# Two FFNs on inputs scaled by the norm's weight alone, the norm's factor applied per token to the gate and up tiles

## The reference, cut to what matters

```python
def rms_norm(x, g):
    xf = x.astype(jnp.float32)
    y = xf * lax.rsqrt(jnp.mean(xf * xf, axis=-1, keepdims=True) + RMS_EPS)
    return (y * g.astype(jnp.float32)).astype(x.dtype)

def swiglu(h, w1, w3, w2):                       # 1024 -> 2816 (gate w1, up w3) -> 1024
    return (jax.nn.silu(h @ w1) * (h @ w3)) @ w2

x = x + 0.5 * swiglu(rms_norm(x, ffn1_norm), ffn1_w1, ffn1_w3, ffn1_w2)      # FFN 1
... # the mixer: projections, RWKV recurrence, attention, gates
x = x + (gate_a * y_a + gate_b * y_b) @ w_out
x = rms_norm(x + 0.5 * swiglu(rms_norm(x, ffn2_norm), ffn2_w1, ffn2_w3, ffn2_w2), final_norm)   # FFN 2
... # the second block, with FFN 3 and FFN 4
```

## Time and profile before

| | |
|---|---|
| runs | 1651.48, 1647.41, 1649.91 us; median 1649.91 |
| the profiled execution | 1648.0 us, span 1646.2 us, mean granted clock 0.997 |
| PE busy | 1627.7 us, 99% of the span |
| DVE busy | 1115.4 us, 68% |
| ACT busy | 698.3 us, 42% |
| POOL busy | 23.9 us, 1% |
| HBM read | 265.38 MB, 162 GB/s over the span |
| chain that ended last | PE 73%, issue 23%, DVE 3%, ACT 1% |
| FFN 1 | about 12 to 204 us |
| output projection | about 452 to 477 us |
| FFN 2 | about 481 to 668 us |

### The profile page before, as it was taken

How to read it: one execution, slowest core, us unless ns; L and a number is a source line. 1 busy time by engine, 2 the same in 40 slices (tenths; PEclk the granted TensorE clock), 3 DMA queues, 4 the chain that set the end, 5 groups by cost and what they waited for, 6 DMA issues and landing times.

```text
span 1646.2 us, 30278 instructions
## 1 busy us (share of the span) xinstructions
PE 1627.7 (99%) x12552; PEld 1477.9 (90%) x12552; DVE 1115.4 (68%) x1617; ACT 698.3 (42%) x918; POOL 23.9 (1%) x41
## 2 busy tenths in 40 slices
PE   9999999999999999999999999999999999999998
PEld 7999888899999999988888887988999999999997
DVE  7666657564887766668887874967457676676665
ACT  6444456434455444421222122516354445454443
POOL 1000000000000000000000000000000000000000
PEclk9999999999999999999999999999999999999998
DMA  7555477322265545243456542233323355545551
GB/s 292 178 188 194 154 283 265 120 79 105 104 237 180 203 178 195 98 158 140 164 193 253 193 166 77 103 128 104 108 77 112 146 183 187 194 154 189 192 180 52
DMA packets 37837, 267.80 MB, mean 163 GB/s; under 512 B 4268, under 2 KB 4524, under 8 KB 5744
## 3 DMA queue, kind: packets, MB, share of 16 engines
q1 hardware_dynamic: 33552, 238.25, 40.5%
q0 software_dynamic: 4192, 28.19, 4.5%
HBM read 265.38 MB, written 1.05 MB: 162 GB/s over the span
## 4 chain that ended last, share of the span: by engine, by line
PE 73%; issue 23%; DVE 3%; ACT 1%; DMA 0%; POOL 0%; POOLq 0%; SPq 0%; DVEq 0%; ACTq 0%
PE PS L436 15%; PE PS L437 15%; PE PS L442 11%; PE PS L655 9%; PE PS L828 6%; PE PS L659 5%; PE PS L684 2%; PE PS L892 1%; DVE W_LO L430 1%; PE PS L540 1%; PE PS L872 1%; PE PS L874 1%; PE PS L873 1%; PE PS L1178 0%; PE PS L1353 0%
## 5 line engine op out<-in xcount | busy, mean ns | idle before, releaser
L430 DVE TENSOR_TENSOR W_LO<-RAW,W_HI 128x2048 fp32r<-128x2048 f32 x210 | 476.2, 2269 | 181.8 <-ACT W_HI L418 180.9
L418 ACT ACTIVATE W_HI<-RAW 128x2048 fp32r<-128x2048 f32 x208 | 397.6, 1913 | 362.1 <-PE PS L442 239.9
L436 PE MATMUL PS<-HS,W_HI 128*128 128x256 f32 (+1 forms) x792 | 265.3, 339 | 1.5 <-ACT G L1732 0.8
L437 PE MATMUL PS<-HS,W_LO 128*128 128x256 f32 (+1 forms) x792 | 261.5, 334 | 0.0
L655 PE MATMUL PS<-HS,W_HI 128*128 128x512 f32 x984 | 246.5, 392 | 0.7 <-DVE W_LO L430 0.7
L442 PE MATMUL PS<-HS,W_HI 128*128 128x512 f32 (+1 forms) x712 | 242.1, 340 | 0.0
L436 PE MATMUL PS<-HID_HI,W_HI 128*128 128x256 f32 (+1 forms) x720 | 220.6, 307 | 0.3 <-DVE XC L2598 0.3
L437 PE MATMUL PS<-HID_HI,W_LO 128*128 128x256 f32 (+1 forms) x720 | 220.2, 307 | 0.0
L655 PEld LDWEIGHTS PS<-HS,W_HI 128*128 128x128 f32 x984 | 177.0, 189 | 32.6 <-DVE W_LO L430 0.9
L436 PEld LDWEIGHTS PS<-HS,W_HI 128*128 128x128 f32 x792 | 150.1, 189 | 19.7 <-issue 3.3
L437 PEld LDWEIGHTS PS<-HS,W_LO 128*128 128x128 f32 x792 | 150.2, 190 | 14.9
(11 more groups left out here) (442 smaller groups left out, 2425.6 us busy)
## 6 DMA issues: line engine op xcount, KB each, us to landing
RAW<-stream SPq DMA_DIRECT2D x225, 1024.0 KB, 4.8
LATE<-stream POOLq DMA_DIRECT2D x24, 1024.0 KB, 5.1
XC<-xin SPq DMA_DIRECT2D x2, 512.0 KB, 4.6
XC<-xin POOLq DMA_DIRECT2D x1, 1024.0 KB, 5.1
out<-NT SPq DMA_DIRECT2D x4, 256.0 KB, 2.6
CON<-consts POOLq DMA_DIRECT2D x1, 616.0 KB, 6.5
LW<-lora POOLq DMA_DIRECT2D x1, 512.0 KB, 6.7
DFT<-dft POOLq DMA_DIRECT2D x1, 266.0 KB, 2.9
```

Of the source, the lines that this page charges most:

```text
L418: nc.scalar.activation(W_HI[s % RING][:], RAW[PLACE[u]][:], ACT.Copy).then_inc(hi_done, 1)
L430: last = nc.vector.tensor_tensor(W_LO[s % RING][:, o], RAW[PLACE[u]][:, o], W_HI[s % RING][:, o].bitcast(F32), ALU.subtract)
L436: nc.tensor.matmul(acc, w_hi, x_hi, start=first, stop=False)
L437: return nc.tensor.matmul(acc, w_lo, x_hi, start=False, stop=last)
```

## The change

In FFN 1 and FFN 2 the matmuls take `x * g`, split into high and low part straight from `XC`; the factor per token is copied once from its PSUM spread to SBUF (`RSF`, `RSC`) and multiplied on DVE onto every gate sum and every up sum (`by_rms`). On the last tile the silu is multiplied once more by the factor in place of the up half. For FFN 1 the rows are made by DVE, eight scalings and eight remainders; the square adds go to POOL, and unit 0's low part goes from POOL to DVE, in halves. For FFN 2 ACT makes the high row `k` behind add `k` and before square `k`, and DVE the low row `m - 1` before add `m`. On PE, the norm sums and the spread move into the first up tile, whose passes are reordered; the sums, scalings, roundings and `keep_clock` matmuls ahead of FFN 2 go, and the wait for `mod_out` moves from before up 2 to before FFN 2. The third and fourth FFN stay as they are.

```diff
@@ gpsimd
-            pool.wait_ge(landed[0], 16)
-            for h in range(2):
-                pool.wait_ge((S("hi_half"), hi_done)[h], 1)
-                ...
-            last.then_inc(lo_done, 1)
+            for k in range(1, NORM_ADDS["na"] + 1):
+                pool.wait_ge(S("norm_sq"), k + 1)
+                if k > 1:
+                    pool.wait_ge(S("norm_acc"), k - 1)
+                nc.gpsimd.tensor_tensor(NT[:, 0], NT[:, 0], NT[:, k], ALU.add).then_inc(S("norm_acc"), 1)
+            pool.wait_ge(landed[PLACE[2]], 16)
@@ tensor, up(t) of ffn
+                    if t == 0 and f < 2:
+                        h0 = KT * NORM_H[h_name]
+                        for w in range(2):
+                            if f == 0 and w:
+                                pe.wait_ge(hi_done, 1)
+                            for k in range(KT):
+                                pe.wait_ge(S("norm_hi"), h0 + k + 1)
+                                c = (w * KT + k) * P
+                                nc.tensor.matmul(tile(w), W_HI[sl][:, c:c + P], H_HI[:, 0, k], start=(k == 0), stop=False)
+                            if f == 0 and w == 0:
+                                norm_sum("na", 0, first=6, last_k=0)
+                        for w in range(2):
+                            for k in range(KT):
+                                pe.wait_ge(S("norm_h"), h0 + k + 1)
+                                c = (w * KT + k) * P
+                                nc.tensor.matmul(tile_lo(w), W_HI[sl][:, c:c + P], H_LO[:, 0, k], start=False, stop=False)
+                            if f == 1 and w == 0:
+                                norm(h_name)
+                        if f == 0:
+                            norm_spread(h_name)
+                        for w in range(2):
+                            ...
+                            for k in range(KT):
+                                c = (w * KT + k) * P
+                                last = nc.tensor.matmul(tile(w), W_LO[sl][:, c:c + P], H_HI[:, 0, k], start=False, stop=(k == KT - 1))
+                            last.then_inc(psum_ready, 1)
+                        if f == 1:
+                            norm_spread(h_name)
+                        return
@@ tensor, before FFN 2
-            norm_sum("nc", 0)
-            norm_sum("nc", 6)
-            keep_clock(1, 0)
-            norm_sum("nc", 7)
-            keep_clock(1, 0)
-            norm_spread("nc")
-            keep_clock(2, 0)
+            pe.wait_ge(S("mod_out"), 1)
@@ scalar, opening
+            act.wait_ge(landed[PLACE[0]], 16)
+            A(W_HI[0][:, 0:UNIT // 2], ...).then_inc(S("half"), 1)
+            A(W_HI[0][:, UNIT // 2:], ...).then_inc(hi_done, 1)
             act.wait_ge(S("par_in"), 16)
             root("na")
-            ...
-            for k in range(KT):
-                round_rows("na", 0, k)
             split_hi(act, 1)
+            act.wait_ge(S("norm_spread"), NORM["na"] + 1)
+            A(RSF[:], spread_of("na"), ACT.Copy).then_inc(S("row_scale"), 1)
@@ scalar, out_square and behind it
-                for k in range(4):
+                for k in range(KT):
+                    if k == 4:
+                        split_hi(act, PHASE[phase] + 5)
+                    if high is not None:
+                        act.wait_ge(S(sem), k + 1)
+                        high(k)
                     square(name, 0, k, sem, k + 1)
-                ...
+            out_square("out", "nc", "x_out1", lambda k: A(H_HI[:, 0, k], XC[:, 0, k], ACT.Identity, scale=par("n2", k)).then_inc(S("norm_hi"), 1))
             root("nc")
-            for k in range(KT):
-                round_rows("nc", 0, k)
+            act.wait_ge(S("norm_spread"), NORM["nc"] + 1)
+            A(RSC[:], spread_of("nc"), ACT.Copy).then_inc(S("row_scale"), 1)
@@ vector, ffn
+                def by_rms(ins, rows_, n_, j=None, j0=0):
+                    ins.then_inc(S("summed"), 1)
+                    dve.wait_ge(S("row_scale"), (1, 3)[f])
+                    n_ += f * (2 * FT - 1)
+                    dve.wait_ge(S("summed"), n_ if j is None else (j - j0) * 4 + n_)
+                    return V.tensor_tensor(rows_, rows_, rms[:], ALU.mult)
 ...
                     if t == FT - 1:
+                        if f < 2:
+                            link(V.tensor_tensor(SILU[:, 1, 0:ROWS], SILU[:, 1, 0:ROWS], rms[:], ALU.mult))
+                            dve.wait_ge(psum_ready, x(mark, 12))
@@ vector, opening
-            for k in range(1, 6):
-                add_squares("na", k)
             dve.wait_ge(S("par_in"), 16)
-            dve.wait_ge(S("con_in"), 16)
+            for k in range(KT):
+                dve.wait_ge(S(f"x_in{k // 4}"), 16)
+                V.tensor_scalar(H_HI[:, 0, k], XC[:, 0, k], par("n1", k), None, ALU.mult).then_inc(S("norm_hi"), 1)
+            for k in range(KT):
+                ...
+                V.scalar_tensor_tensor(out=H_LO[:, 0, k], in0=XC[:, 0, k], scalar=par("n1", k), in1=H_HI[:, 0, k].bitcast(F32), op0=ALU.mult, op1=ALU.subtract).then_inc(S("norm_h"), 1)
             reciprocal("na")
-            norm_rows("na", 0, lambda k: par("n1", k))
-            dve.wait_ge(lo_done, 1)
+            for h in range(2):
+                ...
+                V.tensor_tensor(W_LO[0][:, o], RAW[PLACE[0]][:, o], W_HI[0][:, o].bitcast(F32), ALU.subtract).then_inc(...)
             split_lo(dve, 1)
@@ vector, out_add and behind it
                 for m in range(KT):
                     if m % 2 == 0:
                         split_lo(dve, s0 + m // 2 + 2)
+                    if m and low is not None:
+                        low(m - 1)
                     dve.wait_ge(psum_ready, MARK0[s0] + m + 1)
 ...
+            def low_rows(k):
+                dve.wait_ge(S("norm_hi"), KT * NORM_H["nc"] + k + 1)
+                V.scalar_tensor_tensor(out=H_LO[:, 0, k], in0=XC[:, 0, k], scalar=par("n2", k), in1=H_HI[:, 0, k].bitcast(F32), op0=ALU.mult, op1=ALU.subtract).then_inc(S("norm_h"), 1)
-            norm("nc", 0, lambda k: par("n2", k))
+            out_add("out", [4, 6, 3, 1], lambda m: 1.0, "x_out1", "nc", low=low_rows)
+            reciprocal("nc")
```

More of the change, by code:

```diff
@@ L134 @@
 NORM = {n: k for k, n in enumerate(("na", "nb", "nf", "nc", "nd", "ng", "nh", "ni", "nj"))}
+NORM_T = {n: k for k, n in enumerate(("nb", "nf", "ne", "ng", "nh", "ni"))}
 NORM_H = {n: k for k, n in enumerate(("na", "nb", "nc", "nf", "ne", "ng", "nh", "ni"))}
@@ L604, in up @@
                 def up(t, s, j=None, j0=0):
-                    if t == 0 and f == 0:
-                        pe.wait_ge(hi_done, 1)
+                    if t < 2 and f == 0:
+                        pe.wait_ge(hi_done if t else S("half"), t + 1)
                     else:
@@ L656, in up @@
                                                  start=(k == 0), stop=False)
+                            if t == 1 and f == 0 and w == 0:
+                                wait_unit(s)
                             for k in range(KT):
@@ L902, in _ @@
             pe.wait_ge(S("set_up"), 3)
-            for k in (6, 7, 0):
+            pe.wait_ge(S("con_in"), 16)
+            keep_clock(2, 0)
+            for k in (6, 7):
                 norm_sum("na", k, first=6, last_k=0)
-            pe.wait_ge(S("con_in"), 16)
-            keep_clock(1, 0)
-            norm_spread("na")
             keep_clock(2, 0)
@@ L1846, in out_square @@
                 split_hi(act, PHASE[phase] + 4)
-                for k in range(4):
+                for k in range(KT):
[4 more added lines that the diff above has]
+                        high(k)
                     square(name, 0, k, sem, k + 1)
-                split_hi(act, PHASE[phase] + 5)
-                for k in range(4, KT):
-                    square(name, 0, k, sem, k + 1)
-            out_square("out", "nc", "x_out1")
+            out_square("out", "nc", "x_out1", lambda k: A(H_HI[:, 0, k], XC[:, 0, k], ACT.Identity, scale=par("n2", k)).then_inc(S("norm_hi"), 1))
             root("nc")
-            for k in range(KT):
-                round_rows("nc", 0, k)
+            act.wait_ge(S("norm_spread"), NORM["nc"] + 1)
+            A(RSC[:], spread_of("nc"), ACT.Copy).then_inc(S("row_scale"), 1)
             def round_nf(k0):
@@ L2052, in scale @@
             def scale(name, half, k, gain, dst, sem="norm_t", cols_=None):
-                V.scalar_tensor_tensor(out=dst[:, k], in0=XC[:, half, k], scalar=gain(k), in1=(spread_of(name) if cols_ is None else cols_),
-                                       op0=ALU.mult, op1=ALU.mult).then_inc(S(sem), 1)
+                ins = V.scalar_tensor_tensor(out=dst[:, k], in0=XC[:, half, k], scalar=gain(k), in1=(spread_of(name) if cols_ is None else cols_),
+                                             op0=ALU.mult, op1=ALU.mult)
+                if sem is not None:
+                    ins.then_inc(S(sem), 1)
             def rest(name, half, k, shift=None, tmp=NT):
@@ L2261, in gates, with out_add @@
```

(4 more changed lines are left out.)

59 lines of the change are left out of this document (33 added, 26 removed).

## The result

The changed kernel took 1662.17 us (median of 6 runs, 1660.42 to 1666.29), the kernel before 1650.97 beside it (6 runs, 1647.41 to 1651.56): ratio 1.0077, 95% interval 1.0067 to 1.0087, so it is slower by 11.2 us. The forecast was 1656.0 with a range of 1650 to 1661: the sign was right, the forecast growth of 6.05 was about half of what came, and the time lies above the range. The profiled execution took 1660.84 us, span 1658.8, mean granted clock 0.992 (0.997 before).

The account below looks back on a forecast made before the run. PE, busy 99% of the span, was taken as the bound. FFN 1 (-1.1 + 0.3) and FFN 2 (+5.05 + 1.5 + 0.3) sum to +6.05 us: 1656.0 on the median of 1649.91, range 1650 to 1661.

Parts of the forecast that it names:

- FFN 1, the opening: Start to FFN 1's first down projection: gain of 1.1 us, bounds 0 to 2.8.
- unit 3's high part 24.8: FFN 1's opening: the high part of weight unit 3, behind the Silu at 23.0, ends at 24.8.
- the allowance of 0.35 for POOL beside DVE: FFN 1's opening: POOL's square adds beside DVE's rows may delay the factor, so gain taken as 1.1, not 1.45.
- The clock: Hand-over to FFN 2: without clock-keeping matmuls PE restarts at 1.2 GHz, +1.5 us, bounds 0 and 6.9.
- The hand-over: Output projection to FFN 2's first down projection: late rows 3.3 and the chain behind the spread 1.75, +5.05 us.
- DVE's standstill: Output projection: DVE stands still from 462.0 to 468.25 before low row 0; last add 5.6 us later.
- Rival 1: Hand-over: the clock stays at 2.4 GHz, +4.55 in all, 1654.5 us; chance 0.18.
- The end of each FFN: Last tile of FFN 1 and FFN 2: rounded product 0.3 us late for PE, twice, bounds 0 and 1.8.
- The steady rounds: Rounds of both FFNs: DVE goes from 10.55 to 12.4 of 16.95 us, price 0, up to 0.9 a round.
- Rival 4: Steady rounds: DVE becomes the bound, 20 rounds at up to 0.5 us, 1666; chance 0.07.
- rival 2: Output projection: DVE's standstill costs no time, -0.35 there, about 1649 us in all; chance 0.13.
- Rival 3: Opening and hand-over: PE's own work decides, -2.8 and -2.1 us, 1645; chance 0.05.

Follow-up runs that it names:

- FFN 2 alone: The changed kernel with FFN 1, its norm and its share of the multiplications taken back to the kernel before: 1661.46 us, ratio 1.0067.
- the mended kernel: Changed kernel with low rows last, table loads later, third unit's high part earlier, three clock-keeping matmuls behind FFN 1, two between low rows' matmuls: 1646.09 us, ratio 0.9977.

## Why the prediction was wrong, point by point

**What was missed.** By the medians the change cost 11.2 us where the sum had 6.05. The forecast was laid on a median of three runs, and the six beside the changed kernel lie 1.06 higher. Of the 5.1 us missing in the growth, the two profiles put 2.1 in the opening, 0.9 in the hand-over, 0.5 at the ends of the FFNs and 0.1 in the mixer. The other 1.5 or so are, it seems, half clock in executions other than the profiled one (below): the two slowest of the changed kernel's six runs, 1666.29 and 1665.11, have the lowest mean clocks, 0.990 and 0.991. The 3.01 behind FFN 1 is no part of it: the fall is the kernel before's too, and the 1.9 us by which the prediction went from its profile to the median are about what it costs a median there (1.8).

**The step that failed first: "FFN 1, the opening".** The -1.1 came out as +0.98. It was mis-sized at one link: "unit 3's high part 24.8" took unit 3 as landed. It is issued when the low part of unit 0 is done (16.23 now, 15.39 before), and POOL, rid of that low part, issues its loads from 14.80 on (15.33 in the kernel before): unit 3 goes out 0.8 later and the loads 0.5 earlier, so more of them are ahead of it. Its high part started at 24.89, where the working had it from 23.0 on, and the links behind it moved by that 1.9, the last by 0.4 more. With the loads out of the way the opening gives -0.93, 0.2 from the forecast. That is close by two errors against each other: the allowance of 0.35 for POOL beside DVE was hardly needed (the factor's copy started at 15.77, with 15.65 in the working, though POOL's five adds took 4.59 us and not 3.0), and DVE's seven steps on hidden tile 1 took 3.3 where 2.9 were counted. The Trainium skill ("DMA: Bandwidth & Descriptors", Issuing engines are not separate DMA queues) says that transfers issued by different engines run on the same DMA engines and interleave; the 1.77 us of ACT's wait, gone when only POOL's loads are moved, agrees. The prediction counted POOL's adds and not the DMAs issued behind them.

**The second: "The clock".** It looked for half clock only where the change drops clock-keeping matmuls, and gave that one price. The opening's longer wait on DVE added a place at 33 us, 1.5 where it struck, which the sum had at nothing, and in the hand-over the stretch was twice as long in FFN 2 alone, 48.20 against 44.02. How often each comes in the runs without a profile is not known, so the 1.5 left over are argued, not shown. For the changed kernel's profile 1.3 to 1.6 for 1.5 is right, but partly by luck: the working took 0.26 us a piece at full clock, and the 26 lines in 5.42 us give 0.21, by which the same sum has 2.2. The Trainium skill ("TensorE: Matmul & The Clock Gate", Part 1) calls half rate the default that activity releases; the 0.50 behind PE's idle stretch agrees. It also says that the number of slow matmuls at a kernel's start changes from run to run; here a stretch of half clock in the middle did, with the same instructions around it.

**The fall behind FFN 1** had a row to be seen by: PE idle for 1.31 us and then on narrow norm sums (202.62 above), much as in the tail. The profile shown was one of the executions without it. The prediction named the 1.9 us between its profile and the median and did not ask what they were. Three matmuls in the kernel before say it: the clock.

**The hand-over was right.** DVE's standstill is there (add 0 at 466.43, low row 0 at 472.83 behind ACT's high row), and the last add ended 21.8 after the start of add 0 where the working had 21.5. What ended ACT's wait for unit 4 was no longer the DMA but PE, done with a buffer of high parts (4.82 at 470.48); the two come so close together that the time hardly changed (4.05 behind add 0, 4.34 before). PE was through with the spread 30.66 after add 0, with 30.43 forecast, the clock included. The chain behind took 13.36 instead of 12.85, 0.28 of the difference ACT's start behind the spread. All in all 7.42 for 6.55; 0.16 of the difference is that the forecast counted from the chain's 498.38, and the first matmul of that projection stands at 498.22. Rival 1, a clock that stays up, is out by the 0.50 at 486 to 492.

**The end of each FFN** cost 0.72 and 0.37 for 0.3: a size. On the last tile the gate sum also came 0.37 later.

**The steady rounds** cost nothing, as said: up to the last tile FFN 1's rounds agree to 0.72 us in all, and the mended kernel has all the multiplications and is faster. Rival 4 is out; rival 2 is out by the standstill. Rival 3, that PE's own work decides, is what the mended kernel comes nearer to: -2.05 of its -2.8 in the opening and -1.24 of its -2.1 in the hand-over.

The mixer between them gave 0.10 though the clock fell there too (0.50 at 442 to 444). Other executions with that fall took up to 1.3 us more than this one, those without it 250.1 to 250.9 for its 250.52, so a price there is not settled.

## What to carry to other kernels

Before comparing two profiles, ask why each differs from its median: a stretch of half clock in one and not in the other looks like a cost of the change and need not be one. Look at every stretch in which TensorE idles next to narrow matmuls, as for the 1.31 us behind FFN 1: there the clock differed between executions here, and three dummy matmuls about as long as the idle time settled it. When an engine loses a task, follow what it issues next: DMAs that go out earlier delay those behind them. An input made row by row for the next stage should stand behind the work that frees the present stage, not inside its loop.

## What the runs showed of the hardware

The price of half clock depends on how long it lasts and on what stands behind it. With 0.50 for nearly 7 us it was 2.9 us behind FFN 1 (17.37 against 14.45) and 1.3 to 1.6 in the hand-over; where it lasted about half as long it was 1.4 to 1.6 behind FFN 1 (15.74 to 16.03), and from 486 to 499, in the hand-over of FFN 2 alone, 5.4 to 5.8. With three float32 matmuls, 1.46 us, in the idle stretch behind FFN 1 the clock stayed at 1.00 through the nearly 2 us of narrow norm sums in each of the three profiled executions that have them; the other runs of the kernel before with them have a mean clock of 0.997 or 0.998, and its profiled execution without the fall has 0.997. One such matmul is two lines of the profile and 0.42 us.
